# Output projection of a pooling and gating layer: seven block products in place of eight for chunks 1 and 2

## What is computed

```python
shift, scale, gate = split(silu(c) @ w_ada + b_ada, 3)
h = layer_norm(x) * (1 + scale) + shift
xa, ga, u, v, gb = split(h @ w_in)                  # 1024 -> 5 x 512
ya = pool_mixer(xa, w_pool, pool_scale) * silu(ga)   # causal means over 2, 4, 8, 16 tokens
yb = sgu_mixer(gelu(u), gelu(v), ...) * silu(gb)     # u * (W_s LN(v) + b) in blocks of 128 tokens, 4 heads
y = concatenate([ya, yb]) @ w_out                    # 1024 -> 1024
out = layer_norm(2 ** 0.25 * x + gate * y) * ln_g + ln_b
```

## Time and profile before

| what | value |
|---|---|
| median of 3 runs | 673.7 us (673.05 to 674.21) |
| the profiled execution | 673.68 us, span 671.6 us |
| TensorE, VectorE, ScalarE busy | 98%, 77%, 35% of the span |
| granted TensorE clock, mean | 0.998 |
| DMA moved | 108.73 MB, mean 162 GB/s |

### The profile page before, as it was taken

How to read it: one execution, slowest core, us unless ns; L and a number is a source line. 1 busy time by engine, 2 the same in 40 slices (tenths; PEclk the granted TensorE clock), 3 DMA queues, 4 the chain that set the end, 5 groups by cost and what they waited for, 6 DMA issues and landing times.

```text
span 671.6 us, 8845 instructions
## 1 busy us (share of the span) xinstructions
PE 659.8 (98%) x3103; PEld 551.3 (82%) x3103; DVE 516.1 (77%) x956; ACT 235.1 (35%) x307; POOL 61.7 (9%) x77
## 2 busy tenths in 40 slices
PE   8999999999999999999999999999999999999995
PEld 8888888877888888888888888888888888888884
DVE  5678898749969967766979968775977986656776
ACT  4424644316522333224722332322821333323300
POOL 2000110100002201100002201000002210000010
PEclk9999999999999999999999999999999999999999
DMA  8995643785334472288243562378343454224111
GB/s 340 365 332 233 219 153 116 163 228 189 125 111 141 126 258 86 95 116 322 96 156 100 180 248 65 106 94 332 102 148 90 162 205 159 104 79 154 52 63 62
DMA packets 34546, 108.73 MB, mean 162 GB/s; under 512 B 6573, under 2 KB 7633, under 8 KB 34514
## 3 DMA queue, kind: packets, MB, share of 16 engines
q1 hardware_dynamic: 34514, 108.31, 49.5%
HBM read 97.80 MB, written 10.50 MB: 161 GB/s over the span
## 4 chain that ended last, share of the span: by engine, by line
PE 95%; issue 2%; DVE 2%; ACT 0%; DMA 0%; POOLq 0%; POOL 0%; DVEq 0%
PE bank_b L1053 63%; PE bank_a L1053 25%; PE bank_a L1180 2%; PE bank_a L1140 1%; PE bank_b L1113 1%; PE bank_a L1171 1%; DVE w_low L656 1%; PE bank_b L1077 0%; DVE v_gelu L708 0%; PE bank_b L1171 0%; PE bank_b L1132 0%; PE bank_b L1104 0%; DMA vector_rows<-in_vectors 0%; ACT h_high L528 0%; ACT w_high L509 0%
## 5 line engine op out<-in xcount | busy, mean ns | idle before, releaser
L1053 PE MATMUL bank_b<-h_high,w_high 128*128 128x512 f32 x512 | 202.2, 395 | 0.2 <-DVE h_low L668 0.2
L1053 PE MATMUL bank_b<-h_low,w_high 128*128 128x512 f32 x512 | 199.3, 389 | 0.0
L1053 PE MATMUL bank_b<-h_high,w_low 128*128 128x512 f32 x512 | 199.3, 389 | 0.0
L661 DVE TENSOR_TENSOR w_low<-w_float,w_high 128x1024 fp32r<-128x1024 f32 x98 | 119.5, 1220 | 40.3 <-ACT w_high L518 40.2
L518 ACT ACTIVATE w_high<-w_float 128x1024 fp32r<-128x1024 f32 x98 | 103.4, 1056 | 130.5 <-DMA w_float<-in_w_units 57.2
L1053 PEld LDWEIGHTS bank_b<-h_high,w_high 128*128 128x128 f32 x512 | 96.2, 188 | 20.2 <-issue 1.1
L1053 PEld LDWEIGHTS bank_b<-h_high,w_low 128*128 128x128 f32 x512 | 96.1, 188 | 20.1
L1053 PEld LDWEIGHTS bank_b<-h_low,w_high 128*128 128x128 f32 x512 | 96.2, 188 | 19.5 <-issue 0.5
L461 POOL TENSOR_TENSOR z_rstd<-z_var_eps,minus_half 128x1 f32<-128x1 f32 x16 | 22.0, 1377 | 361.8 <-DVE z_var_eps L905 351.9
L1053 PE MATMUL bank_a<-w_high,y_high 128*128 128x512 f32 x128 | 49.9, 390 | 0.2 <-issue 0.2
L1053 PE MATMUL bank_a<-w_high,y_low 128*128 128x512 f32 x128 | 49.8, 389 | 0.0
(11 more groups left out here) (180 smaller groups left out, 934.0 us busy)
## 6 DMA issues: line engine op xcount, KB each, us to landing
w_float<-in_w_units SPq DMA_DIRECT2D x90, 512.0 KB, 3.4
x_norm<-in_x SPq DMA_DIRECT2D x16, 512.0 KB, 4.5
z<-in_x SPq DMA_DIRECT2D x16, 512.0 KB, 5.2
out<-z SPq DMA_DIRECT2D x15, 512.0 KB, 4.8
z<-in_mod_units SPq DMA_DIRECT2D x12, 512.0 KB, 9.1
x_norm<-in_x_channels SPq DMA_DIRECT2D x12, 512.0 KB, 15.0
w_float<-xa_units SPq DMA_DIRECT2D x12, 512.0 KB, 3.5
mod_spare<-in_mod_units SPq DMA_DIRECT2D x6, 512.0 KB, 8.6
```

What stands on the lines that cost most here:

```text
L661: vec.tensor_tensor(wL[:, n % S_SLOTS, :], w_float(c, n), wH[:, n % S_SLOTS, :].bitcast(F32), ALU.subtract).then_inc(w_low, 1)
L1053: last = mm(bank, wl if n == 2 else wh, ml if n == 1 else mh, start=start and n == 0, stop=stop and n == 2)
```

## The change

For chunks 1 and 2 (`FAST`) the output is computed in the form of seven products of blocks in place of eight (Strassen's scheme with Winograd's sums). y is cut by tokens (two halves of 256) and by channels (pooling and gating part), the weights by rows and by columns.

- **Sums of weights.** In chunk 0 and the first steps of chunk 1, VectorE multiplies the output weights by the gate (`gate_weights`) and forms their sums (`sum_weights`), one group of rows at a time; SyncE loads each group (2 x 512 KB) and stores seven pieces of 256 KB (`prep_load`, `prep_store`) to memory. These are the output's units later.
- **Sums of y.** After each group of chunk 1 and 2 VectorE forms four sums over 256 columns (`sums_of_y`); two of them are split at once, two late, at steps 25 to 28 (`late_low`).
- **Products.** Product i is two units of 12 matmuls each (`fast_unit`), so the output has 14 units, and the chunk 34. Products 4, 5 and 6 go on adding into banks that products 2 and 3 have filled and VectorE has read. After product i VectorE adds the banks of its parts to z (`add_parts`), without the gate, which is in the weights. Statistics of z come afterwards (`z_stats_of`).
- **Landing.** Two more slots, in the v tile, for half of the output's units.
- **Order.** In these chunks x's statistics are taken at steps 8 to 11, its rows stored at 12, its channels loaded at 12 to 15, normalised at 16 to 19; the h parts stand at steps 22 to 32.
- The hardware loop over chunks 1 and 2 is written out. All low parts are made by VectorE, as before.

Of the diff (empty lines left out):

```diff
+FAST = (1, 2)
+PRODUCTS = 7
+FAST_UNITS = IN_UNITS + 2 * PRODUCTS
+PARTS = ((0, 0, 0, 0), (0, 1, 1, 0), (1, 2, 2, 0), (1, 3, 3, 0), (2, 4, 0, 0), (2, 5, 1, 0), (3, 6, 2, 1), (3, 7, 3, 1),
+         (4, 4, 0, 1), (4, 5, 1, 1), (5, 6, 0, 1), (5, 7, 1, 1), (6, 4, 2, 1), (6, 4, 2, 0), (6, 5, 3, 1), (6, 5, 3, 0))
+READ_IN = {IN_UNITS + 3 + 2 * i: i for i in range(PRODUCTS - 1)}
+LATE_IN = {25: 0, 26: 1, 27: 2, 28: 3}
+PREP_LOAD_IN = {(0, 18): 0, (0, 19): 1, (0, 27): 2, (1, 6): 3}
+GATE_IN = {(0, 23): 0, (0, 26): 1, (1, 2): 2, (1, 8): 3}
+SUMS_IN = {(0, 24): 0, (0, 27): 1, (1, 4): 2, (1, 9): 3}
+PREP_STORE_IN = {(0, 25): 0, (1, 1): 1, (1, 6): 2, (1, 11): 3}
...
+FAST_X_STATS_IN = {8: 0, 9: 1, 10: 2, 11: 3}
+FAST_X_ROWS_IN = 12
+FAST_X_CENTRE_IN = {16: (0, 1), 17: (2, 3), 18: (4, 5), 19: (6, 7)}
+FAST_H_IN = {22: (0,), 23: (1,), 24: (2,), 26: (3,), 28: (4,), 29: (5,), 30: (6,), 32: (7,)}
...
-            with eng.Fori(1, CHUNKS - 1) as c:
-                chunk(c, False, False)
-            chunk(CHUNKS - 1, False, True)
+        def run_chunks(chunk):
+            for c in range(CHUNKS):
+                chunk(c, c == 0, c == CHUNKS - 1)
...
+        def landing(c, n):
+            if c == 0 and n in XA_ALONE:
+                return None
+            if c in FAST and n >= IN_UNITS and (n - IN_UNITS) % 4 >= 2:
+                return F_SLOTS + n % F_SLOTS
+            return n % F_SLOTS
...
+        def prep_tile(q, half):
+            if q in (0, 2):
+                return mS[:, half, :]
+            if q == 1:
+                return gv[:, 2 * half:2 * half + 2, :].rearrange("p j t -> p (j t)")
+            return z[:, half, :]
+        def prep_sums(q):
+            return (wS[:, :], wpF[:, :]) if q < G - 1 else (z[:, 2, :], z[:, 3, 0:T])
...
+            def prep_load(q):
+                if q == 0:
+                    sp.wait_ge(w_low, XA_ALONE[-1] + 1)
+                if q == 1:
+                    sp.wait_ge(sgu_done, G)
+                if q == 2:
+                    sp.wait_ge(out_stored, PRODUCTS * 16)
+                if q == G - 1:
+                    for j in range(TILES):
+                        sp.wait_ge(z_stored[j], 16)
+                for half in range(2):
+                    sp.dma_start(prep_tile(q, half), w_units[IN_UNITS + half * G + q]).then_inc(prep_landed[half], 16)
+            def prep_store(q):
+                sp.wait_ge(prep_ready, q + 1)
+                zero, one, (t12, t4) = prep_tile(q, 0), prep_tile(q, 1), prep_sums(q)
+                for i, half_unit in enumerate((zero[:, 0:T], t4, zero[:, T:], t12[:, 0:T], t12[:, T:], one[:, 0:T],
+                                               one[:, T:])):
+                    cut = slice(q % 2 * T, (q % 2 + 1) * T)
+                    sp.dma_start(out_units[i, q // 2][:, cut], half_unit).then_inc(out_stored, 16)
...
+                        if n == ys_in[g] and c in FAST:
+                            act.wait_ge(ys_ready, c * G + g + 1)
+                            nc.scalar.activation(aH[:, g, :], mixed[:, 0:T // 2], ACT.Copy)
+                            act.wait_ge(s12_ready, FAST.index(c) * G + g + 1)
+                            nc.scalar.activation(yH[:, G + g, :], s12, ACT.Copy).then_inc(ys_high, 1)
+                    if c in FAST and n in LATE_IN:
+                        g = LATE_IN[n]
+                        act.wait_ge(unit_done, base(c) + IN_UNITS + 4)
+                        act.wait_ge(s34_ready, FAST.index(c) * G + g + 1)
+                        nc.scalar.activation(yH[:, g, :], s34[:, g, :], ACT.Copy).then_inc(s34_high, 1)
...
+                if c in FAST and src is mixed:
+                    vec.tensor_tensor(aL[:, g, :], mixed[:, 0:T // 2], aH[:, g, :].bitcast(F32), ALU.subtract)
+                    src = s12
                 vec.tensor_tensor(yL[:, row, :], src[:, :], yH[:, row, :].bitcast(F32), ALU.subtract).then_inc(low, 1)
+            def late_low(c, g):
+                dve.wait_ge(s34_high, FAST.index(c) * G + g + 1)
+                vec.tensor_tensor(yL[:, g, :], s34[:, g, :], yH[:, g, :].bitcast(F32), ALU.subtract).then_inc(s34_low, 1)
+            def gate_weights(q):
+                dve.wait_ge(gate_ready, 2)
+                prep_steps.begin(q)
+                for half in range(2):
+                    rows = prep_tile(q, half).rearrange("p (b n) -> p b n", b=2)
+                    gate = gateB[:, half * HALF:(half + 1) * HALF].rearrange("p (o n) -> p o n", o=1)
+                    dve.wait_ge(prep_landed[half], (q + 1) * 16)
+                    done = vec.tensor_tensor(rows, rows, gate.broadcast_to([P, 2, T]), ALU.mult)
+                prep_steps.then(dve, done)
+            def sum_weights(q):
+                zero, one, (t12, t4) = prep_tile(q, 0), prep_tile(q, 1), prep_sums(q)
+                b21, b11, b22, b12 = zero[:, 0:T], zero[:, T:], one[:, 0:T], one[:, T:]
+                if 0 < q < G - 1:
+                    dve.wait_ge(out_stored, q * PRODUCTS * 16)
+                prep_steps.then(dve, vec.tensor_tensor(t12[:, 0:T], b12, b11, ALU.subtract))
+                prep_steps.then(dve, vec.tensor_tensor(t12[:, T:], b22, t12[:, 0:T], ALU.subtract))
+                vec.tensor_tensor(t4, b21, t12[:, T:], ALU.subtract)
+                vec.tensor_tensor(b12, b22, b12, ALU.subtract).then_inc(prep_ready, 1)
+            def sums_of_y(c, g):
+                nth, half = FAST.index(c) * G + g, T // 2
+                if nth == 0:
+                    dve.wait_ge(out_stored, (G - 1) * PRODUCTS * 16)
+                dve.wait_ge(ys_ready, c * G + g + 1)
+                a12, a22 = y_float(c, g)[:, 0:half], y_float(c, g)[:, half:]
+                a11, a21 = mixed[:, 0:half], mixed[:, half:]
+                vec.tensor_tensor(s12[:, 0:half], a21, a22, ALU.add).then_inc(s_steps, 1)
+                vec.tensor_tensor(s34[:, g, 0:half], a11, a21, ALU.subtract)
+                dve.wait_ge(s_steps, nth + 1)
+                vec.tensor_tensor(s12[:, half:], s12[:, 0:half], a11, ALU.subtract).then_inc(s12_ready, 1)
+                dve.wait_ge(s12_ready, nth + 1)
+                vec.tensor_tensor(s34[:, g, half:], a12, s12[:, half:], ALU.subtract).then_inc(s34_ready, 1)
+            def add_parts(c, i):
+                nth = FAST.index(c) * len(PARTS)
+                dve.wait_ge(unit_done, base(c) + IN_UNITS + 2 * i + 2)
+                for p, (product, bank, j, half) in enumerate(PARTS):
+                    if product != i:
+                        continue
+                    cut = slice(half * HALF, (half + 1) * HALF)
+                    psum = (A, B)[bank // 4][:, bank % 4, :]
+                    earlier = [o for o in range(p) if PARTS[o][2:] == (j, half)]
+                    if earlier:
+                        dve.wait_ge(part_read, nth + earlier[0] + 1)
+                        ins = vec.tensor_tensor(z[:, j, cut], psum, z[:, j, cut], ALU.add)
+                    else:
+                        dve.wait_ge(z_landed[j], (c + 1) * 16)
+                        ins = vec.scalar_tensor_tensor(out=z[:, j, cut], in0=z[:, j, cut], scalar=ALPHA, in1=psum,
+                                                       op0=ALU.mult, op1=ALU.add)
+                    ins.then_inc(part_read, 1)
...
+                    if c in FAST and n in READ_IN:
+                        add_parts(c, READ_IN[n])
...
+            def fast_unit(c, w, i, r):
+                nth = FAST.index(c)
+                if r == 0 and i == 0:
+                    pe.wait_ge(v_gelu, (c + 1) * TILES)
+                if r == 0 and i == 1:
+                    pe.wait_ge(ys_summed, (c + 1) * G)
+                if r == 0 and i in (2, 3):
+                    for _, freed in banks_of_group[2 * (i - 2):2 * (i - 1)]:
+                        pe.wait_ge(freed, (c + 1) * G)
+                if r == 0 and i >= 4:
+                    pe.wait_ge(part_read, nth * len(PARTS) + 2 * i - 2)
+                bank0 = (0, 2, 4, 6, 4, 6, 4)[i]
+                for qq in range(2):
+                    q = 2 * r + qq
+                    if i == 0:
+                        pe.wait_ge(yp_low, c * G + q + 1)
+                    if i == 2:
+                        pe.wait_ge(ys_low, c * G + q + 1)
+                    if i == 5:
+                        pe.wait_ge(s34_low, nth * G + q + 1)
+                    high, low, at = ((yH, yL, q), (yH, yL, q), (aH, aL, q), (yH, yL, G + q), (yH, yL, G + q), (yH, yL, q),
+                                     (yH, yL, q))[i]
+                    col = (0, 2, 0, 0, 2, 2, 0)[i] * P
+                    block = slice(qq * T, (qq + 1) * T)
+                    for t in range(2):
+                        psum = (A, B)[bank0 // 4][:, bank0 % 4 + t, :]
+                        cut = slice(col + t * P, col + (t + 1) * P)
+                        done = product(psum, high[:, at, cut], low[:, at, cut], w[0][:, block], w[1][:, block],
```

(52 more changed lines are left out.)

198 lines of the change are left out of this document (133 added, 65 removed).

## The result

The changed kernel takes 695.33 us (693.05 to 695.99, 4 runs) against 673.38 (673.03 to 674.21, 4 runs) of the kernel before beside it: ratio 1.0318 (95% interval 1.0292 to 1.0344). It is slower, as predicted (0.62 on slower), but by 22 us where 7 were forecast, and 7 us above the stated range. The four runs of the changed kernel lie 2.9 us apart, those of the kernel before 1.2, so a difference of 2 or 3 us between single runs of its edits says little without the trace.

What follows compares the result with a forecast made beforehand. The prediction took TensorE, busy 98% of the span, to bound the kernel, with VectorE's added work exceeding its lead and causing stalls. Its sum was 673.7 - 10.9 + 15.6 + 2.2 = 680.6 us, range 667 to 688.

Steps and rivals of the forecast that it cites:

- (c): Chunk 1's unit 13: x tile wait 3.6 us, unit 10's load 1.1; shift 18.05, stall so far 7.9 us.
- (d): Chunk 1's output units 21 to 23: row store's wait taken as 2.7 us; stall 15.6 us by unit 23.
- What bounds the kernel: TensorE, busy 98% of the span, one matmul per 0.2267 us; VectorE makes low parts ahead by a lead.
- What is removed: Output of two chunks: 168 matmuls in place of 192 each, 48 x 0.2267 = 10.9 us less.
- Prices on VectorE: VectorE: 1.13 us per 1024 columns, 0.72 or 0.60 per 512; weights 5.05 per group, 20.2 in all.
- (a): Chunk 1's start, waiting for chunk 0's last addition to z from bank A: stall 1.8 us.
- (b): Low part of chunk 1's unit 8: VectorE shift 9.45 us, stall so far 4.6 us.
- (e): Rest of the output after unit 23: steps 25 to 28 take 10.7 against 10.9 us; stall neither grows nor shrinks.
- (f): Chunk 2's unit 23: stall 2.2 us (none to 5); unrolled loop costed at nothing.
- The clock: Rival: TensorE's clock falls to 1.2 GHz after each stall, up to 38 us, 690 to 719; chance 4%.
- The range: Whole kernel: 667 to 688 us, leaving out most of the all-hidden rival and the clock; own case 675 to 686.
- Markers: Right: 48 matmuls fewer, w_low holes, VectorE over 95% busy; wrong: DMA holes, chunk 2 holes above 5 us, clock below 1.00.

Runs made afterwards that it cites:

- edit 1: Changed kernel with SyncE loading the x tile ahead of the stores and loads of the weight sums: 694.94 us.
- edit 3: Changed kernel with the four sums of y formed on 2 columns in place of 256: 691.16 us.
- edit 4: Changed kernel with 4 to 14 filler matmuls of 128 columns on constants before each of the ten late units: 690.30 us.
- edit 9: Changed kernel, both fast chunks, with x's normalisation of channels 6 and 7 moved to steps 29 and 31 of the output: 687.97 us.
- edit 11: Changed kernel with gating and weight sums on one column, stores of 4 columns, units loaded from plain weights, and x's normalisation spread: 670.54 us.
- edit 2: Changed kernel with gating and weight sums done on one column in place of 1024 or 512, loads, stores and waits kept: 676.51 us.
- edit 5: Changed kernel with the 28 weight-sum stores moving 4 columns in place of 512, output units loaded from the plain weights: 686.73 us.
- edit 6: Changed kernel with the weights' gating and sums, 32 operations of 128x512, moved to GpSimd in chunk 0's output: 696.12 us.
- edit 7: On top of edit 6, the subtraction of x's mean in chunks 1 and 2 also runs on GpSimd: 695.56 us.
- edit 12: On edit 9, the 28 stores of the weight sums are issued by GpSimd in place of SyncE: 685.38 us.

## Why the prediction was wrong, step by step

Three terms failed, and none of them is a price of work: the wait for the x tile (c), the wait around the row store (d), and half pace, costed at nothing. Together they are 14.6 of the 15.4 us missed.

- **What bounds the kernel, and the mechanism: right.** The added VectorE work uses up the lead of the low parts, and holes wait for w_low at units 8, 12, 13 and 21 to 23 as named; the first, at chunk 1's start, came as well. Units 17 and 20 were not named.
- **What is removed: right**, 48 matmuls.
- **Prices on VectorE: right.** A pair of gating operations takes 2.35 us (2.4 predicted with its gap), the sums stand 0.73, 0.72, 0.61 and 0.60 apart, at 194.14 to 196.80:

```profile
194.14 0.69 DVE L1042 TENSOR_TENSOR w_spare<-v_gelu 128x512 f32<-128x512 f32 x1 [0.87 <-DMA out_units<-mod_spare]
194.87 0.69 DVE L1043 TENSOR_TENSOR w_spare<-v_gelu,w_spare 128x512 f32<-128x512 f32 x1
195.59 0.69 DVE L1044 TENSOR_TENSOR w_pool<-v_gelu,w_spare 128x512 f32<-128x512 f32 x1
196.20 0.68 DVE L1045 TENSOR_TENSOR v_gelu<-v_gelu 128x512 f32<-128x512 f32 x1
196.80 0.69 DVE L1109 TENSOR_TENSOR tanh<-bank_a,gate_rows 128x512 f32<-128x512 f32 x1
```

- **(a) and (b): right**, 1.9 for 1.8 and 4.3 for 4.6. The wait for the first stores, costed at nothing and at most 2, was 0.87. A ledger of work, idle time and lead gave both as long as work was all that was added. That it did so within 0.3 us is luck: in edits 1, 3, 4 and 9, whose programs are the same up to chunk 1's start, that start is 1.2 to 3.4 us late, and unit 8 is 3.6 to 5.8 late.
- **(c) mis-sized**: late at unit 13 by 11.8 where it said 7.9. The two new waits were put at 1.1 and 3.6; they were

```profile
248.73 1.23 DVE L800 TENSOR_TENSOR w_low<-w_float,w_high 128x1024 fp32r<-128x1024 f32 x1 [2.03 <-ACT w_high L640]
...
257.67 1.29 DVE L820 BATCH_NORM_STATS2 x_stats<-x_norm 128x6 f32<-128x512 f32 x2 [7.12 <-DMA x_norm<-in_x]
```

  so 9.15 in place of 4.7: 4.4 more, against 3.9 missed. The tile landed 13.8 us after the first store was issued (243.87 to 257.64). The rate did not fail: in that time the queues moved 4.67 MB, 339 GB/s in the mean, which is the slower end that I had allowed (340). What failed is what the 3.85 MB were taken to be. For the first 1.4 us the queues moved 119 GB/s at most, and 0.8 MB of the 4.67 belong to loads issued behind the tile, which travelled beside it. The issue too was dearer, 6.3 for nine where nine times 0.38 is 3.4. The rule of the Trainium skill that the forecast weighed (DMA: Bandwidth & Descriptors, Queues, rings and completion order) is not contradicted: the tile did land late, though edit 1 shows that its place in the order is not what costs.
- **(d) wrong in its reasoning**, the largest miss. It put the wait around the row store at 2.7, "VectorE is late itself by then and asks later, so only a part of it is felt". The rows have it in full, 3.18 and 5.65:

```profile
296.36 1.23 DVE L800 TENSOR_TENSOR w_low<-w_float,w_high 128x1024 fp32r<-128x1024 f32 x1 [3.18 <-ACT w_high L640]
...
304.73 1.23 DVE L800 TENSOR_TENSOR w_low<-w_float,w_high 128x1024 fp32r<-128x1024 f32 x1 [5.65 <-ACT w_high L640]
```

  8.8 us, as the 8.6 of before. The forecast also took the wrong load for the cause. These waits are for units 16 and 17, and SyncE's timeline has their loads, then unit 18's:

```profile
285.17 0.70 SPq L406 DMA_DIRECT2D w_float<-xa_units  x1
...
290.13 0.34 SPq L406 DMA_DIRECT2D w_float<-in_w_units  x1
...
299.32 0.65 SPq L406 DMA_DIRECT2D w_float<-in_w_units  x1
```

  The first two were issued before SyncE stood waiting for the row store (until 298.05) and took 10.0 and 13.4 us to land. They travelled beside it: from 290.5 to 298.0, with the row store under way, the queues moved 27 GB/s at a DMA share of 81%. Only unit 18's load was held back in SyncE's program; VectorE waits 0.70 for it. The kernel before shows the same (14 GB/s from 290.5 to 298.2). The 8.63 us there are for unit 21, but its load is not the one issued at 300.05, as the forecast read the earlier trace rows; that is unit 22's. Unit 21's went out before the wait and took 16.2 us to land:

```profile
290.57 3.20 SPq L316 DMA_DIRECT2D w_float<-in_w_units  x1
```

  By this reading the row store holds up VectorE twice: it slows the loads beside it, and it keeps back the next one. The chain of waits goes through the second (286.53, 299.32). By it VectorE could not have begun unit 18's low part before 308.63, even with units 16 and 17 there at once. No run takes the row store away, so its share is read from the traces.

  Why lateness didn't help: the row store follows VectorE's last statistics (they end at 283.56, GpSimd's x_rstd at 285.10, SyncE issues at 285.92 and 286.53), and unit 17's load follows VectorE's low part of unit 15 (290.11). When VectorE is late, both are late by about as much: a wait at the end of a chain that starts at the waiting engine isn't shortened by that engine's lateness. Edit 11, where the same wait is 8.2 us and no hole stands ahead of the output, agrees; in edits 2 and 5 the two waits come to 5.4 and 5.9 only, so their size is not a constant. From unit 13 to 23 13.9 us were lost where 7.7 were forecast, 6.2 more; the wait is 6.1 of them.
- **(e) nearly right**: no hole after unit 23 in chunk 1.
- **(f) a little low**: 3.7 us of holes for 2.2, inside its 0 to 5.
- **The clock: costed at nothing**, and as a rival at 4% with 690 to 719. The mechanism came, with a granted clock of 0.59 in the stretch above. Its size is given by edit 4, one run: 5.0 us net. The Trainium skill, TensorE: Matmul & The Clock Gate, Part 1, has the clock gated down after idleness; I gave that little because no stretch of the kernel before showed a short hole. That was a reason not to know, and no reason against.
- **The range** failed because its high end allowed 5.0 for each of the two waits, where they were 7.1 and 8.8, and left out the clock. For the second no row gave the 5.0, and the earlier trace rows already had 8.63. The misses, unit 8's -0.3 among them, are -0.3 + 4.2 (unit 13) + 6.2 + 1.5 (f) + 4.2 (clock) - 0.4 (less time around the span) = 15.4, which is 695.99 of the profiled execution less 680.6.
- **Markers.** Right: 48 matmuls, the first hole, the w_low holes, VectorE's wait for the x tile. Wrong: VectorE over 95% busy up to step 13 (15 of 24 us from 233.2 on), and "a granted clock below 1.00" occurred.

What stays open is which holes are followed by half pace (none after the 3.3 us at 272.14, one after the 2.3 at 280.00). It was not tried why the x tile's wait stays at 5.4 us with the stores' bytes gone, nor what the kernel takes with the row store out of the way.

## What to carry to other kernels

A ledger of lead, idle time and added work prices the work well. Price each wait by the chain that ends it: if that chain begins at the engine that waits, lateness doesn't shorten it. Before a wait is put down to a load, match the load with its unit; the one issued last before the wait ends need not be it. When a saving on the bounding engine is paid with work on a feeder that is itself nearly full, first look where the work can be put: here 24 matmuls saved with the same preparation spread over two chunks gain 4.9 us, and 48 saved with it pressed into one stretch lose 22. The holes here, 23.4 us in sum, brought 8.2 us of half pace with them, of which 5.0 were felt, so a marginal trade of matmuls for stalls is a bad one.

## What the hardware showed that was not expected

- Half-pace spells of 3 to 4 us behind holes of only 2 to 3 us, 1.6 to 1.7 us lost in each; dummy matmuls in the holes prevent all of them (edit 4).
- Beside GpSimd, VectorE's two-input operations in SBUF take 1.77 for 0.69 us and 2.31 for 1.22: moving work there gained nothing (edits 6 and 7; there VectorE also waits 10.5 us for z_rstd).
- Stores of 256 KB in a row take SyncE up to about 1 us each to issue, against 0.43 for the first; from GpSimd beside a row store they take 14.6 us to land (edit 12).
- A store of 2 KB that turns a column into a row takes 11.5 us to land (286.53 to 298.05), and SyncE stands behind it. While it and its fellow were under way the queues moved 27 GB/s from 290.5 to 298.0, and a load of 512 KB issued at 290.13 took 13.4 us to land.
